# A hybrid decoder layer on one Trainium2 core: the triangular inverse of each DeltaNet head built from blocks of 4 instead of 16

## What is computed

```python
cum_g = jnp.cumsum(g, axis=-1)
decay_mat = jnp.exp(jnp.where(causal, cum_g[..., :, None] - cum_g[..., None, :], -jnp.inf))
kk = jnp.einsum("nbhid,nbhjd->nbhij", k, k)
a_mat = jnp.where(strict, beta[..., :, None] * kk * decay_mat, 0.0)
rhs = jnp.concatenate([v * beta[..., None], k * (beta * jnp.exp(cum_g))[..., None]], axis=-1)
sol = lax.linalg.triangular_solve(eye + a_mat, rhs, left_side=True, lower=True,
                                  unit_diagonal=True)
```

## Time and profile before

| | us |
|---|---|
| median of 3 runs | 1641.9 (1641.84 to 1643.56) |
| the profiled execution, time | 1643.32 |
| the profiled execution, span | 1641.8 |
| PE busy | 1592.5 |
| PEld busy | 1316.3 |
| DVE busy | 1092.7 |
| ACT busy | 790.1 |
| POOL busy | 158.3 |

### The profile page before, as it was taken

The page is one execution under the profiler, slowest core; times in us unless marked ns, Lnnn a source line. Parts: engine busy times, 40 slices in busy tenths (PEclk is TensorE's granted clock), DMA queues, the critical chain, the costliest instruction groups (busy, mean ns, idle before and its releaser), DMA issues.

```text
span 1641.8 us, 20823 instructions
## 1 busy us (share of the span) xinstructions
PE 1592.5 (97%) x7858; PEld 1316.3 (80%) x7858; DVE 1092.7 (67%) x1320; ACT 790.1 (48%) x1048; POOL 158.3 (10%) x154
## 2 busy tenths in 40 slices
PE   6999999999999999999999999999999999999997
PEld 5888888887887887887887887888888778777885
DVE  5745745645646646556568758867677999888863
ACT  5434534435434444335335346556465845447442
POOL 4101001001001000010011011011010000001011
PEclk9999999999999999999999999999999999999999
DMA  8304314223223233133143337576566556775653
GB/s 261 78 26 115 84 38 129 57 76 90 77 57 99 73 77 96 51 89 83 51 113 101 137 136 210 192 192 220 140 189 187 196 196 209 202 217 112 196 116 52
DMA packets 192379, 206.19 MB, mean 126 GB/s; under 512 B 7491, under 2 KB 139846, under 8 KB 190726
## 3 DMA queue, kind: packets, MB, share of 16 engines
q1 hardware_dynamic: 176470, 161.69, 33.2%
q0 software_dynamic: 15856, 43.80, 11.2%
HBM read 180.28 MB, written 29.38 MB: 128 GB/s over the span
## 4 chain that ended last, share of the span: by engine, by line
PE 81%; issue 6%; DVE 5%; DMA 5%; ACT 2%; POOL 1%; SPq 0%; ACTq 0%; POOLq 0%; DVEq 0%
PE bank L740 14%; PE bank L744 14%; PE bank L742 14%; PE bank L1161 8%; PE bank L1163 8%; PE bank L1165 8%; PE bank L769 6%; DMA e_block<-branch_a 2%; PE bank L774 1%; DVE ring_lo L2117 1%; PE bank L930 1%; PE bank L946 1%; DMA operands<-branch_a 1%; ACT ring_hi L1520 1%; PE bank L940 1%
## 5 line engine op out<-in xcount | busy, mean ns | idle before, releaser
L740 PE MATMUL bank<-h_hi_r,w_hi 128*128 128x512 f32 x1008 | 421.5, 418 | 0.0
L744 PE MATMUL bank<-h_hi_r,w_raw_r 128*128 128x512 f32 x1008 | 396.9, 394 | 0.0
L742 PE MATMUL bank<-h_lo_r,w_hi 128*128 128x512 f32 x1008 | 394.1, 391 | 0.0
L2117 DVE TENSOR_TENSOR ring_lo<-operands,ring_hi 128x1024 fp32r<-128x1024 f32 x224 | 271.8, 1221 | 117.8 <-ACT ring_hi L1520 116.8
L1520 ACT ACTIVATE ring_hi<-operands 128x1024 fp32r<-128x1024 f32 x224 | 235.5, 1059 | 230.0 <-PE bank L1165 174.4
L744 PEld LDWEIGHTS bank<-h_hi_r,w_raw_r 128*128 128x128 f32 x1008 | 189.1, 188 | 43.0
L742 PEld LDWEIGHTS bank<-h_lo_r,w_hi 128*128 128x128 f32 x1008 | 190.3, 189 | 35.6 <-issue 1.7
L740 PEld LDWEIGHTS bank<-h_hi_r,w_hi 128*128 128x128 f32 x1008 | 189.9, 188 | 35.8 <-issue 1.7
L1161 PE MATMUL bank<-ring_hi,h_hi_r 128*128 128x512 f32 x480 | 190.6, 397 | 3.1 <-issue 3.1
L1163 PE MATMUL bank<-ring_lo,h_hi_r 128*128 128x512 f32 x480 | 189.4, 395 | 0.0
L1674 DVE TENSOR_TENSOR w_raw_r<-w_raw,w_hi 128x2048 fp32r<-128x2048 f32 x64 | 146.7, 2292 | 45.9 <-ACT w_hi L1219 44.7
(11 more groups left out here) (324 smaller groups left out, 2179.4 us busy)
## 6 DMA issues: line engine op xcount, KB each, us to landing
w_raw<-in_w_in_dram SPq DMA_DIRECT2D x64, 1024.0 KB, 6.0
operands<-in_w_in_dram SPq DMA_DIRECT2D x64, 512.0 KB, 4.7
operands<-in_w_o_dram SPq DMA_DIRECT2D x32, 512.0 KB, 4.9
operands<-in_w_in_dram POOLq DMA_DIRECT2D x16, 512.0 KB, 8.7
gates<-e_block POOLq DMA_DIRECT2D x16, 512.0 KB, 5.3
operands<-in_w_out_gdn_dram SPq DMA_DIRECT2D x16, 512.0 KB, 4.0
operands<-gates SPq DMA_DIRECT2D x16, 512.0 KB, 5.2
operands<-in_w_out_moba_dram SPq DMA_DIRECT2D x16, 512.0 KB, 4.6
```

Of the source, the lines that this page charges most:

```text
L740: pe.matmul(PJ[slot % 2][:], w_hi[slot % 2][:, c], h_hi[:, k, :], start=(k == 0), stop=False, skip_group_check=True)
L742: pe.matmul(PJ[slot % 2][:], w_hi[slot % 2][:, c], h_lo[:, k, :], start=False, stop=False, skip_group_check=True)
L744: mm = pe.matmul(PJ[slot % 2][:], w_lo[slot][:, c], h_hi[:, k, :], start=False, stop=(k == KT - 1), skip_group_check=True)
L2117: dve.tensor_tensor(ring_lo[:, n % RINGS, :], operand(q, p, j), ring_hi[:, n % RINGS, :].bitcast(F32), ALU.subtract).then_inc(s["op_lo"], 1)
```

## The change

- `LEVELS = (4, 8, 16, 32, 64)`: the diagonal blocks are of 4, one squaring (`n1`, then one product `n2`) inverts them, and five merges (`ma`/`mb` 0 to 4) follow instead of three. Merge k with b = LEVELS[k] works on m = 128 - b rows and weight columns, and on the 64 moving columns that belong to the second block of each pair; the products of all other columns are masked or not made. The last merge (64) is as before. TensorE's products of 128 weight columns per head go from 48 to 8, and 32 with 64 moving columns and m weight columns come in; the turns stay 16 (plus the four for v).
- The second orientation of the decay, `dL`, is computed: three DVE operations of 512 columns in `cgrow` instead of four of 128, one more exponential on ACT, and four POOL operations (`decay_parts`) instead of one in the opening of the head. `UT` and `LT` go, and POOL's two masked copies too. The row that POOL fetches from DRAM has twice the bytes (a row of -beta beside the decay).
- In head 0 four more products (-beta as rows) and one more transposition on TensorE, one ACT copy, and on DVE nine small operations that make the masks (`level_masks`), ahead of `split(n + 2, 2)`.
- DVE's operations of the merges are of 256 columns. `vTs` and the wait for its result (`vb`) move behind merge 3; the wait stands ahead of one step of window 4. `split`, `silu(h, 2)`, `conv(h, 2)`, `zclamp`, `zmul` and the last head's steps are placed anew between the merges.

```diff
+LEVELS = (4, 8, 16, 32, 64)
+NL = len(LEVELS)
+PAIRED = P // 2
...
+        def half_tile(ap, t, b, which):
+            return ap[:, tile4(t)].rearrange("p (n s b) -> p n s b", s=2, b=b)[:, :, which, :]
...
             def decay_row(h):
 
                 pool.wait_ge(s["cg_eg"], h)
-                pool.wait_ge(s["cg_arg"], 4 * h)
-                pool.dma_start(cgb[:], cg_dram[bass.ds(h, 1), :].broadcast_to([P, T])).then_inc(s["cg_rows"], 16)
+                pool.wait_ge(s["cg_arg"], 3 * h)
+                pool.wait_ge(s["cg_dts"], 4 * h)
+                pool.dma_start(rows2[:], cg_dram[bass.ds(h, 1), :, :].broadcast_to([P, 2, T])).then_inc(s["cg_rows"], 16)
+            def decay_parts(h):
+                pool.wait_ge(s["cg_dl"], h + 1)
+                pool.tensor_tensor(q4(dL), q4(dL), hcb(HC_NB), ALU.mult).then_inc(s["cg_dts"], 1)
+                pool.wait_ge(s["masks"], 2 * NL - 1)
+                pool.wait_ge(s["Ud"], h)
+                pool.wait_ge(s["n2_mm"], h)
+                pool.tensor_tensor(q4(dTb), q4(dT), over(masked4), ALU.mult).then_inc(s["cg_dts"], 1)
+                pool.wait_ge(s["Ld"], h)
+                pool.wait_ge(s["cg_dts"], 4 * h + 1)
+                pool.tensor_tensor(q4(dLm), q4(dL), over(masked4), ALU.mult).then_inc(s["cg_dts"], 1)
+                if not (isinstance(h, int) and h == 0):
+                    pool.wait_ge(s["cg_rows"], 16 * (NT + h))
+                pool.wait_ge(s["cg_dts"], 4 * h + 2)
+                pool.tensor_tensor(dTb[:], dTb[:], nb_row, ALU.mult).then_inc(s["cg_dts"], 1)
 
             def head(h, p):
 
                 if p is not None:
                     decay_row(h)
-                pool.wait_ge(s["cg_dt"], h + 1)
-                pool.wait_ge(s["n3_mm"], h)
-                pool.tensor_tensor(q4(dTs), q4(dT), over(plane(C_STRICT)), ALU.mult).then_inc(s["cg_dts"], 1)
+                decay_parts(h)
...
-                pool.wait_ge(s["Ln"], h + 1)
-                pool.wait_ge(s["ma_mm"], 3 * h)
-                pool.tensor_tensor(q4(lm[1]), q4(Ln), over(plane(C_L32)), ALU.mult).then_inc(s["L32m"], 1)
-                pool.tensor_tensor(q4(lm[2]), q4(Ln), over(plane(C_L64)), ALU.mult).then_inc(s["L64m"], 1)
...
+                for t in range(NT):
+                    mm = pe.matmul(G1[:, tile4(t)], hcol[:, HC_NB, t:t + 1].broadcast_to([P, P]), ident[:],
+                                   start=True, stop=True)
...
-            def UT(h):
-                pe.wait_ge(s["kkd"], h + 1)
-                pe.wait_ge(s["kdec"], h + 1)
-                turn(G0, Up).then_inc(s["UT_mm"], 1)
-            def LT(h):
-                pe.wait_ge(s["Ln"], h + 1)
-                turn(G2, Ln).then_inc(s["LT_mm"], 1)
             def n1(h):
                 pe.wait_ge(s["Ud"], h + 1)
                 pe.wait_ge(s["Ld"], h + 1)
-                pe.wait_ge(s["qkd"], h + 1)
-                four(G0, Ud, Ld)
-                four(G1, Ld, Ud).then_inc(s["n1_mm"], 1)
+                pe.wait_ge(s["kdec"], h + 1)
+                four(G0, Ud, Ld).then_inc(s["n1_mm"], 1)
 
             def n2(h):
                 pe.wait_ge(s["L2"], h + 1)
-                pe.wait_ge(s["U2"], h + 1)
                 pe.wait_ge(s["X1"], h + 1)
-                four(G0, U2, L2)
-                four(G1, L2, U2)
+                pe.wait_ge(s["Ln"], h + 1)
                 four(G2, L2, xa).then_inc(s["n2_mm"], 1)
...
+                b = LEVELS[k]
                 if k == 0:
-                    pe.wait_ge(s["X8"], h + 1)
-                    pe.wait_ge(s["L8"], h + 1)
-                    pe.wait_ge(s["vb"], h + 1)
-                elif k == 1:
-                    pe.wait_ge(s["X"], 3 * h + k)
-                if k < 2:
-                    pe.wait_ge((s["L32m"], s["L64m"])[k], h + 1)
-                    four(G0, lm[k + 1], src)
-                    mm = turn(G1, src)
-                else:
+                    pe.wait_ge(s["X2"], h + 1)
+                    pe.wait_ge(s["qkd"], h + 1)
+                elif k < NL - 1:
+                    pe.wait_ge(s["X"], NL * h + k)
+                if k == NL - 1:
                     for t in range(NT):
...
+                else:
+                    m = P - b
+                    for t in range(NT):
+                        pe.matmul(G0[:m, t * PAIRED:(t + 1) * PAIRED], Ln[:, t * P:t * P + m],
+                                  half_tile(xa, t, b, 1), start=True, stop=True)
+                    for t in range(NT):
+                        mm = pe.transpose(G1[:m, t * P:t * P + m], xa[:m, t * P:t * P + m], ident[:m, :m])
                 mm.then_inc(s["ma_mm"], 1)
...
+                    m = P - LEVELS[k]
+                    for t in range(NT):
+                        mm = pe.matmul(G2[:m, t * PAIRED:(t + 1) * PAIRED], XTt[:m, t * P:t * P + m],
+                                       Yt[:m, t * PAIRED:(t + 1) * PAIRED], start=True, stop=True)
...
-                UT(h)
+                n1(h)
                 win(2, 12, 14)
                 ss(h, 1)
-                win(2, 14, 15)
-                LT(h)
-                win(2, 15, 16)
-                win(3, 0, 1)
+                win(2, 14, 16)
+                n2(h)
+                win(3, 0, 2)
                 qk(h)
-                win(3, 1, 4)
-                n1(h)
-                win(3, 4, 7)
-                n2(h)
-                win(3, 7, 10)
-                n3(h)
-                win(3, 10, 13)
-                n4(h)
-                win(3, 13, 16)
+                win(3, 2, 5)
+                ma(h, 0)
+                win(3, 5, 8)
+                mb(h, 0)
+                win(3, 8, 11)
+                ma(h, 1)
+                win(3, 11, 14)
+                mb(h, 1)
+                win(3, 14, 16)
+                win(4, 0, 1)
+                ma(h, 2)
+                win(4, 1, 4)
+                mb(h, 2)
+                win(4, 4, 7)
+                ma(h, 3)
+                win(4, 7, 10)
+                mb(h, 3)
+                win(4, 10, 12)
                 vTs(h)
-                win(4, 0, 2)
-                ma(h, 0)
-                win(4, 2, 5)
-                mb(h, 0)
-                win(4, 5, 8)
-                ma(h, 1)
-                win(4, 8, 11)
-                mb(h, 1)
-                win(4, 11, 13)
-                pe.wait_ge(s["X"], 3 * h + 2)
+                win(4, 12, 13)
+                pe.wait_ge(s["X"], NL * h + NL - 1)
+                pe.wait_ge(s["vb"], h + 1)
                 win(4, 13, 14)
-                ma(h, 2)
+                ma(h, 4)
                 win(4, 14, 16)
-                pe.wait_ge(s["Y"], 3 * h + 3)
-                pe.wait_ge(s["XT"], 3 * h + 3)
+                pe.wait_ge(s["Y"], NL * h + NL)
+                pe.wait_ge(s["XT"], NL * h + NL)
                 win(5, 0, 1)
-                mb(h, 2)
+                mb(h, 4)
...
+                act.wait_ge(s["cg_arg"], 3 * h + 2)
                 act.activation(dT[:], dT[:], ACT.Exp).then_inc(s["cg_dt"], 1)
+                act.wait_ge(s["cg_arg"], 3 * h + 3)
+                act.activation(dL[:], dL[:], ACT.Exp, scale=-1.0).then_inc(s["cg_dl"], 1)
...
-                for t in range(NT):
-                    dve.scalar_tensor_tensor(dT[:, tile4(t)], row[:, tile4(t)], hcol[:, HC_CG, t:t + 1],
-                                             plane(C_DMASK), ALU.subtract, ALU.add).then_inc(s["cg_arg"], 1)
+                dve.tensor_tensor(q4(dL), q4(row), hcb(HC_CG), ALU.subtract).then_inc(s["cg_arg"], 1)
+                dve.wait_ge(s["cg_arg"], 3 * h + 1)
+                dve.tensor_tensor(q4(dT), q4(dL), over(plane(C_DMASK)), ALU.add).then_inc(s["cg_arg"], 1)
+                dve.tensor_tensor(q4(dL), q4(dL), over(plane(C_CMASK)), ALU.subtract).then_inc(s["cg_arg"], 1)
...
-                dve.wait_ge(s["cg_dts"], h + 1)
-                dve.wait_ge(s["mb_mm"], 3 * h)
-                dve.tensor_tensor(Up[:], G2[:], dTs[:], ALU.mult).then_inc(s["kkd"], 1)
-            def UT(h):
-                dve.wait_ge(s["UT_mm"], h + 1)
-                dve.wait_ge(s["ma_mm"], 3 * h)
-                dve.tensor_tensor(q4(Ln), q4(G0), hcb(HC_NB), ALU.mult).then_inc(s["Ln"], 1)
-            def LT(h):
-                dve.wait_ge(s["LT_mm"], h + 1)
+                dve.wait_ge(s["cg_dts"], 4 * h + 4)
                 dve.wait_ge(s["o_mm"], 4 * h)
-                dve.tensor_tensor(q4(Ud), q4(G2), over(plane(C_M16)), ALU.mult).then_inc(s["Ud"], 1)
+                dve.tensor_tensor(Ud[:], G2[:], dTb[:], ALU.mult).then_inc(s["Ud"], 1)
                 dve.wait_ge(s["o_out"], 16 * h)
-                dve.tensor_tensor(q4(Ld), q4(Ln), over(plane(C_M16)), ALU.mult).then_inc(s["Ld"], 1)
+                dve.tensor_tensor(Ld[:], G2[:], dLm[:], ALU.mult).then_inc(s["Ld"], 1)
+            def kk_rest(h):
                 dve.wait_ge(s["Ud"], h + 1)
+                dve.wait_ge(s["vn_mm"], 4 * h)
                 dve.tensor_tensor(q4(xa), q4(Ud), over(ident[:]), ALU.add).then_inc(s["X1"], 1)
```

(102 more changed lines are left out.)

144 lines of the change are left out of this document (62 added, 82 removed).

## The result

The changed kernel takes 1647.3 us (median of 7 runs, 1644.7 to 1648.7), the kernel before 1641.9 in the same comparison (7 runs, 1640.6 to 1643.6): a ratio of 1.0031, 95% interval 1.0019 to 1.0043. It is slower by 5.4 us, a third of a per cent and clear of the noise, and the forecast was 1646.6. The profiled execution took 1647.9 us against the 1648.0 of the sum.

The account below looks back on a forecast made before the run. TensorE, its matmuls busy 97% of the span, bounds the kernel. Heads 1 to 6 -6.4, head 0 +3.5, last head +7.6: +4.7 on 1643.3 profiled gives 1648.0, less 1.4 for the median: 1646.6 us; range 1641 to 1652.

Parts of the forecast that it names:

- Head 0: First head: +3.5 us, bounds +1.6 and +5.3, including 1.3 for late columns and 3.3 for later waits.
- the opening: Start of heads 1 to 7: longer DVE decay work and POOL delay TensorE by 1.05 us, bounds 0.8 and 2.3.
- the inverse: TensorE, per head: fewer records save 1.78 us and fewer weight columns 0.70, together -2.48 us.
- the last head: Head 7: +7.6 us, bounds 0 and 9; waits of 4.7 at merge 3 and 2.6 for v, clock loss 1.7.
- Rival 1: Products with 64 moving columns: halving these columns halves the work, 18 us saved, 1628 us; chance 0.08.
- "+0.05 us" for POOL: Opening of heads 1 to 7: DVE's softmax scaling falls near the end of POOL's first operation, costing 0.05 us.
- rival 3: Opening of seven heads: DVE's scaling waits for two POOL operations, 1.25 us more each, +9, 1655 us; chance 0.12.
- The wait for v: Middle of each head: TensorE waits before a window 4 step for scaled v, +0.37 us, bounds 0.2 and 0.6.
- Heads 1 to 6: Inverse, opening and wait for v together: -1.06 us each, -6.4 us in all.
- DVE and POOL take turns: Head 0: with the two engines alternating, TensorE waits 2.2 us at k's turn and 2.9 at n1; 3.3 taken.
- Rival 2: Head 0 and last head: collisions missed and store early, only +1.6 and +1.2, sum -3.6, 1638.3 us; chance 0.25.
- Everything after the heads is untouched.: Stage behind the heads: no change, since its waits follow TensorE's own progress.

Follow-up runs that it names:

- run 10: The kernel before, with its four decay operations moved into DVE's gap behind the second softmax scaling: 1639.4 us against 1640.3, ratio 0.9996.
- 9: Changed kernel with decay in DVE's gap, last head's row sums later, v turned earlier, head 0's masks early and decay on DVE: 1619.1 us, ratio 0.9870.
- run 4: Changed kernel, first product of each merge of levels 4 to 32 with 128 moving columns instead of 64: 1652.5 us, ratio 1.0070.
- 5: Changed kernel, merge products and transpositions of levels 4 to 32 with all 128 weight columns, moving columns still 64: 1654.9 us, ratio 1.0087.
- run 3: The kernel before, with DVE doing its four decay operations twice in heads 1 to 7: 1650.8 us, ratio 1.0048.
- run 1: Changed kernel, POOL's four decay operations held until DVE has written the first scaled softmax tile, heads 1 to 7: 1640.3 us, ratio 0.9992.
- run 8: Changed kernel, v turned one window step earlier: 1646.5 us, ratio 1.0031.
- Run 6: Changed kernel, steps 8, 9 and 10 of the row sums placed later on DVE in the last head: 1641.0 us, ratio 0.9997.
- run 2: Changed kernel, DVE's decay operations moved into its gap behind the second softmax scaling, ACT's exponentials and POOL's operations later too: 1634.1 us, ratio 0.9958.
- run 7: Changed kernel, in head 0 masks built before the first convolution and POOL's decay operations after the second: 1649.0 us, ratio 1.0042.

## Why the forecast came out right, and what in it was wrong

The total was right to 0.7 us, and that is luck: none of its parts was. By the three marks I had +4.55, -6.4, +6.55 and nothing behind; the profile has +6.2, -2.9, +3.7 and -2.5. Head 0 and the opening were too cheap, the inverse and the last head too pessimistic. What was right is the kind of loss: waits at the opening, for v and at both ends that eat up a real saving of TensorE.

- **The inverse, -2.48 a head: it is -3.04** (run 10 against 9). The reason for the price was half right. I said that moving columns don't count and that fewer weight columns do. Runs 4 and 5 show that the slower of the two counts, so the gain from the shrinking loads exists only because the moving columns were halved. I also gave the transpositions no gain; they fall from 0.35 to 0.28. The two products of 32 moving columns could not tell this, since their load was full. In run 4 the full moving columns of one half of the merges' products cost 0.5 us a head.
- **Rival 1** (half the moving columns, 18 us) did not happen: 0.05 us for eight records is what they save alone (0.89 to 0.84).
- **The opening, +1.05: it is +1.85** in seven heads (4.27 us of windows against 2.42). DVE's part was right: 0.88 more for its three operations, and run 3 shows no slack. The step that failed is "+0.05 us" for POOL. I let the scaling fall near the end of POOL's first operation. It fell 0.09 us after the start of the second and waited for all of it: 0.97 (run 1). This is rival 3, at 0.97 instead of 1.25 and with only 0.12 of chance; its own sentence, that the four stand in a row with no gap, was the one to trust. By the Trainium skill (SBUF — State Buffer, section Who interferes with whom) whoever issues first keeps the shared pair for its whole instruction, and a DVE tensor_scalar can be among those that need it; the rows agree for this one (1.26 us for 0.29). They do not for head 0, where DVE's operation began 0.79 us before POOL's first and still stood for all four.
- **The wait for v, +0.37: it is 0.51** for the six window products (1.98 against 1.47), 0.42 by the period (run 8), within its bounds. In my sum v was there 1.38 us after its turn; the rows give 1.33.
- **Heads 1 to 6, -1.06 each: -0.75** (117.72 to 116.97), and one stretch at 1.2 GHz, 1.6 us, which I had not expected behind a wait of 1.8.
- **Head 0.** To head 1's turn of k I had +4.55 (3.5 and one opening), measured +6.2. The columns' spreading came 0.8 us late, not 1.3. The turn of k waited 4.8 us, not 2.2. The step that failed here is that DVE and POOL take turns: of DVE's three convolution steps (7.66 us) one stood for POOL's four operations in a row, 6.09 us. The kernel before had the sign of it in head 0 (2.52 us beside one operation), which I had not used. The first product waited not at all, because k had been late already. The clock took 1.6 more.
- **The last head.** From its turn of k I had +6.55, measured +3.7. The wait for merge 3 was as worked out: 4.7 in the weight load (4.2 at the matmul), since the store landed 7.0 us after its issue and I had taken 7.0. Run 6 shows the cause. The 2.6 us for v did not come: TensorE ran at 1.2 GHz just then and DVE caught up. The clock cost some 2.7 us, not 1.7 (the same records against run 6, start to start, as far as the wait for v).
- **Rival 2** (both ends give way) did not happen.
- **"Everything after the heads is untouched."** The program is, but the stage of some 635 us took between 632.8 and 638.1 us in the twelve profiles, without order in what was changed, and with two to four stretches at 1.2 GHz in it. That is the size of the whole effect here; a single profile can't settle 0.2%.

## What to carry over

A restructuring that saves on the engine that bounds the kernel pays only where each result it needs is early: here 3.0 us of TensorE time per head were real, and one DVE chain longer by 0.9 us, one POOL operation in its way and two crowded ends took them back. Before moving elementwise work to another engine, lay the two engines' timelines over each other and place the work in a measured gap; the same operations moved to such a gap turned +5.4 us into -7.2, and the four repairs together into -21.2. For a small product, cut weight columns and moving columns together: here the longer of the two was what was paid.

## What the runs showed that I had not expected

- A tile operation of DVE with a scalar per partition (128 by 128, 0.29 us) stood still for the whole of a POOL operation that had begun 0.09 us before it. That is one of POOL's operations in a row of four. In head 0 an operation of DVE begun before such a row stood for all four (6.09 us for 0.75), in seven of seven profiles; in run 2 the same kind of operation and POOL's took turns (1.3 to 1.7 us each, beside 1.7 of POOL's). The runs don't show what decides between the two, so the safe price of an operation of DVE beside a row of POOL's is the whole row. The same pair of engines also met the other way round (POOL 3.35 us beside DVE's split, run 7).
- Waits of 1.8 us at the opening were followed by about 3.5 us at 1.2 GHz in 8 of 42 cases (six profiles with this wait, seven each), at 1.6 us a time; waits of 0.9 to 1.2 us never (14 cases, too few to say that they can't be), nor openings with a wait of 0.2 us or none (28 cases). I can't say which of the 42 it takes.
